# Placement of the expert stage's weight pieces and of its turned activations in SBUF: 32 and 256 bytes past multiples of 512

## The reference, cut to what matters

```python
def swiglu(x, w1, w3, w2):
    return (jax.nn.silu(x @ w1) * (x @ w3)) @ w2

def moe_swiglu(x, router, w1, w3, w2):
    ...
    logits = (xt @ router).astype(F32)
    top_v, top_i = lax.top_k(logits, TOP_K)
    gates = jax.nn.softmax(top_v, axis=-1)
    combine = jnp.sum(jax.nn.one_hot(top_i, N_EXPERTS, dtype=F32) * gates[..., None], axis=1)
    out = jnp.zeros(xt.shape, F32)
    for e in range(N_EXPERTS):
        out = out + combine[:, e:e + 1] * swiglu(xt, w1[e], w3[e], w2[e]).astype(F32)
```

## Time and profile before

| | |
|---|---|
| median of three runs | 1508.27 us |
| profiled execution, its own time | 1508.43 us |
| its span, first to last instruction | 1506.6 us |
| granted TensorE clock, mean over the span | 0.995 |
| PE busy | 1479.1 us (98%) |
| weight loads (PEld) busy | 1297.6 us (86%) |
| DVE busy | 1236.9 us (82%) |
| ACT busy | 962.0 us (64%) |
| read from memory, written | 446.45 MB, 36.87 MB |

### The profile page before, as it was taken

The page is one execution under the profiler, slowest core; times in us unless marked ns, Lnnn a source line. Parts: engine busy times, 40 slices in busy tenths (PEclk is TensorE's granted clock), DMA queues, the critical chain, the costliest instruction groups (busy, mean ns, idle before and its releaser), DMA issues.

```text
span 1506.6 us, 23455 instructions
## 1 busy us (share of the span) xinstructions
PE 1479.1 (98%) x8803; PEld 1297.6 (86%) x8804; DVE 1236.9 (82%) x906; ACT 962.0 (64%) x693; POOL 83.8 (6%) x65
## 2 busy tenths in 40 slices
PE   9998999999999999999999999999999999999997
PEld 8987899999999978888888888888888888888885
DVE  6898866656578779889888888888888888988987
ACT  6644353333353567777777777777777777777774
POOL 1035200000000030000000000000000000000300
PEclk9999999999999999999999999999999999999998
DMA  8745697888654669999999999999999999999990
GB/s 311 225 131 157 221 342 267 305 297 300 228 182 168 228 227 413 403 367 389 376 381 382 373 393 375 377 385 376 382 392 359 387 395 361 388 385 364 407 413 36
DMA packets 212938, 483.97 MB, mean 321 GB/s; under 512 B 8810, under 2 KB 26314, under 8 KB 209820
## 3 DMA queue, kind: packets, MB, share of 16 engines
q1 hardware_dynamic: 209224, 473.67, 85.2%
q10 hardware_dynamic: 2388, 5.32, 1.0%
q0 software_dynamic: 1280, 4.33, 0.7%
HBM read 446.45 MB, written 36.87 MB: 321 GB/s over the span
## 4 chain that ended last, share of the span: by engine, by line
PE 86%; DVE 1%; issue 0%; ACT 0%; DVEq 0%
PE Q L2544 20%; PE Q L2495 14%; PE Q L2497 14%; PE Q L2496 14%; PE Q L2039 7%; PE Q L2040 7%; PE Q L2041 7%; PE Q L2528 2%; DVE wlo L1174 1%; PE Q L2474 0%; PE Q L2505 0%; ACT yrows L1149 0%; PE Q L2400 0%; PE Q L2408 0%; PE Q L2032 0%
## 5 line engine op out<-in xcount | busy, mean ns | idle before, releaser
L1174 DVE TENSOR_TENSOR wlo<-raw,whi 128x2048 fp32r<-128x2048 f32 x413 | 940.3, 2297 | 186.2 <-ACT whi L988 109.3
L988 ACT ACTIVATE whi<-raw 128x2048 fp32r<-128x2048 f32 x336 | 642.2, 1919 | 169.8 <-PE Q L2497 81.1
L2495 PE MATMUL Q<-whi,xgh 128*128 128x512 f32 x896 | 354.2, 395 | 0.0
L2497 PE MATMUL Q<-whi,xgl 128*128 128x512 f32 x896 | 349.6, 390 | 0.0
L2496 PE MATMUL Q<-wlo,xgh 128*128 128x512 f32 x896 | 348.9, 389 | 0.0
L2039 PE MATMUL Q<-xh,whi 128*128 128x264 f32 x1024 | 294.7, 288 | 5.4 <-DVEq L1285 1.8
L2040 PE MATMUL Q<-xl,whi 128*128 128x264 f32 x1024 | 292.0, 285 | 0.0
L2041 PE MATMUL Q<-xh,wlo 128*128 128x264 f32 x1024 | 290.7, 284 | 0.0
L2039 PEld LDWEIGHTS Q<-xh,whi 128*128 128x128 f32 x1024 | 193.8, 189 | 8.1 <-issue 4.1
L2497 PEld LDWEIGHTS Q<-whi,xgl 128*128 128x128 f32 x896 | 168.1, 188 | 35.8
L2496 PEld LDWEIGHTS Q<-wlo,xgh 128*128 128x128 f32 x896 | 168.5, 188 | 33.6
(11 more groups left out here) (286 smaller groups left out, 1138.8 us busy)
## 6 DMA issues: line engine op xcount, KB each, us to landing
raw<-in_moe_w SPq DMA_DIRECT2D x336, 1024.0 KB, 7.1
raw<-in_ffn_w SPq DMA_DIRECT2D x42, 1024.0 KB, 7.3
raw<-in_hgrn_w_in SPq DMA_DIRECT2D x16, 1024.0 KB, 7.3
xg_rows<-zeros SPq DMA_DIRECT2D x6, 2048.0 KB, 10.9
y_rows<-zeros SPq DMA_DIRECT2D x6, 2048.0 KB, 11.7
raw<-in_conv_w_in SPq DMA_DIRECT2D x12, 1024.0 KB, 5.4
raw<-in_hgrn_w_out SPq DMA_DIRECT2D x4, 1024.0 KB, 5.0
raw<-in_conv_w_out SPq DMA_DIRECT2D x4, 1024.0 KB, 5.1
```

The lines of the kernel that those rows point to most:

```text
L988: a.activation(bufs(q)[0], raw[:, n % RAW, PW * (q % 2):PW * (q % 2 + 1)], ACT.Copy).then_inc(hi_done, 1)
L1174: v.tensor_tensor(low, raw[:, slot, PW * half:PW * (half + 1)], high.bitcast(F32), ALU.subtract).then_inc(lo_done, 1)
L2495: t_.matmul(out, xgh[:, kt, :], high[:, w], start=(kt == 0), stop=False)
L2497: mm = t_.matmul(out, xgl[:, kt, :], high[:, w], start=False, stop=(kt == DT - 1))
```

## The change

Two tiles are moved. An unused tile `gap` of 64 floats (256 bytes) goes in ahead of `hth`, so that `hth`, `htl` and the small routing tiles behind them begin 256 bytes later. `hs_at`, from which the places of `hs`, `xg`, `xgh` are counted back, is corrected by the same amount and stays. `W2_AT`, the beginning of `whi2`, is put 32 bytes past the rounded value; the rounding itself gives the same number as before, since another area ends later (`conv_end`). So `whi2` and `wlo2`, and with them all blocks in slots 3 to 5, begin 32 bytes past a multiple of 512, as does `gffn`, which uses part of the same space earlier.

```diff
-        (xs, xgh, xgl, xg, hs, hx, hth, htl), o = region(
+        (xs, xgh, xgl, xg, hs, hx, _, hth, htl), o = region(
             R0, ("xs", [P, TT, D], F32), ("xgh", [P, DT, P], F32R), ("xgl", [P, DT, P], F32R),
-            ("xg", [P, D], F32), ("hs", [P, FW], F32), ("hx", [P, FW], F32),
+            ("xg", [P, D], F32), ("hs", [P, FW], F32), ("hx", [P, FW], F32), ("gap", [P, 64], F32),
             ("hth", [P, 4, P], F32R), ("htl", [P, 4, P], F32R))
-        hs_at = o - 2 * size([P, 4, P], F32R) - 2 * size([P, FW], F32)
+        hs_at = o - 2 * size([P, 4, P], F32R) - 2 * size([P, FW], F32) - size([P, 64], F32)
...
-        W2_AT = (max(o, conv_end) + 511) // 512 * 512
+        W2_AT = (max(o, conv_end) + 511) // 512 * 512 + 32
```

## The result

The median went from 1506.74 us (six runs, 1505.57 to 1510.22) to 1519.69 us (six runs, 1517.25 to 1521.66): a ratio of 1.0086 with a 95% interval from 1.0075 to 1.0097, 13.0 us slower. The forecast was 14.2 us slower. The sign, the place and nearly the size came out as written; the reason given for the price did not, as the experiments show.

A forecast was written before the change was run, and what follows sets the result against it. The prediction took PE's matmul rate in the expert stage to bound the kernel; 1508.43 us plus 14.2 for whi2 and wlo2, all else at nothing, gave 1522.6 us, with an 8-in-10 range of 1507 to 1529.

The forecast's parts named there:

- What bounds the kernel: Expert stage: PE is busy 910.00 of 910.00 us, so a matmul's gain or loss moves the end one for one.
- The price of whi2 and wlo2: Up matmuls in slots 3 to 5: 7.08 ns more on each of 2004, 14.2 us, all on PE.
- The reason: Moving operands come in fixed 64-byte groups, 17 steps each, paid in full; a 32-byte offset touches one more, 7.08 ns.
- G: Moving operands: fixed 64-byte groups, each started one paid in full; 32 bytes off gives 561 steps in place of 544.
- the prediction's own list: Expert matmuls: right if slots 3 to 5 stand at 233 to 236 ns and slot 2 and all of down at 226.7.
- hth and htl: Held operands of 1320 down matmuls, 256 bytes on: costed at 0, bounds 0 to 5.0 ns each (6.6 us).
- The one called faster: Expert matmuls: the offset ends load and stream collisions, 13.4 ns each, 44.5 us less, about 1464 us; chance 0.07.
- The one called slower still: Expert matmuls: load and stream kept from settling, 16.6 us on top of 14.2, about 1539 us; chance 0.08.
- No change: Expert streams: groups counted from the operand's own start, 32 for 512 columns wherever they begin; 1508.4 us, chance 0.30.
- The Trainium skill's rule: SBUF operands: cachelines of 16 bytes with a penalty at each crossing, so the change would cost nothing, 1508.4 us.

The follow-up runs named there:

- everything at 32: whi, wlo, whi2, wlo2, xgh, xgl, hth and htl all 32 bytes past a multiple of 512, against the kernel before: ratio 1.0000 (0.9990 to 1.0009).
- slot 2 with `xgh` at 32: whi2, wlo2, xgh and xgl 32 bytes past a multiple of 512, against the kernel before: ratio 1.0026, slot 2 at 233.3 ns.
- the one kernel with 256 columns: The kernel with whi2, wlo2 at 32 bytes and 8 held columns, up streaming 256 of each 512 columns: slot 2 at 115.8 ns, slot 4 at 112.7.
- the control with 8 held columns: The kernel before, all operands at multiples of 512, with up holding 8 of 128 columns of xgh and xgl: ratio 0.9996 (0.9985 to 1.0006).

## Why the prediction was right in size and wrong in its reason

**What bounds the kernel: right.** PE's distances were the time: of the 12.5 us that the span grew, 11.9 lie between the first up and the last down matmul, and PE has no idle time there (920.00 of 920.00 us from 580 on). DVE and ACT only waited longer (114.3 for 104.9 us, 83.4 for 78.4).

**The price of whi2 and wlo2: near in size.** 7.08 ns were forecast for a matmul; settled runs show 6.0 to 6.9. In a block 36 of them are 255 ns, and 217 were measured. The most of what is missing is in slot 3, the first piece behind the transposes: it was unsettled and dear before the change (231.7 ns), so it lost 33 ns a block where 85 were counted; slots 5 and 4 lost 76 and 80 of 85. The prediction had that row and used it for a bound only. Against it stands a loss that it costed at nothing, the head of down, 27 ns a block, where the offsets change over. It also left out 12 down matmuls of the last expert's last block, whose weights lie in slot 5, which are under 0.1 us.

**The reason: wrong.** The step that failed is the one that reads "512 columns that begin half way into one touch 33 groups, not 32". Streams that begin there cost 226.5 ns if the held operand begins there too (everything at 32: ratio 1.0000), streams that begin at a multiple of 512 cost 233.3 if it doesn't (slot 2 with `xgh` at 32), and at 64 bytes, where G asks nothing, 5.4 us were paid. What the runs show in its place is the difference of the two operands' offsets. A sign of it stood in the result already: by the prediction's own list, down that moves too means load against stream, and the first five matmuls of down moved to 232 ns. That 17 steps for a half-used group fitted both 512 and 264 columns was no proof: I took one rule for both because it gave both numbers, and 121.5 ns was a mean of unequal distances; with `fh` and `fl` at multiples of 512 they come apart into 121.7 and 116.7. The size came out by coincidence.

**hth and htl: right, by the right row.** `yh` against `yl` had the same difference of 256 and no price; 0.9991 and 0.9997 confirm it on either side. That row held only for a settled run, though: the same pairing takes 233 ns at the end of the changed kernel (last section).

**The rivals.** The one called faster had the right variable, the difference of offsets, and the wrong sign: equal offsets were the cheap case already. The one called slower still named the mechanism that the runs support (an offset that keeps load and stream from settling) but put it on top of the groups. "No change" fell with the result. The Trainium skill's rule in "SBUF — State Buffer", section "Specifications (TRN2)", lines of 16 bytes, would have every offset here cost nothing. 233.6 ns at 32 and 229.1 at 64 don't agree with it as the only unit, while everything at 32 does.

**What stays open.** Why the difference matters. It isn't in proportion to what is loaded (231.8 ns with 8 columns), with streams of 256 columns the sign turned, and the same offsets have two prices (233.6 and 229.1 ns by turns with 192; 231.1 ns in a row of 71 and 226.7 afterwards with equal offsets). So the price is that of a state which lasts, and the difference of offsets bears on which state a run falls into. That fits a question of when two reads begin against each other, but no run here shows such a time; this was not settled.

## What to carry to other kernels

Where fp32r matmuls of 512 columns follow one another without idle time, compare the offsets of the held and the streamed operand within 512 bytes: equal ones and those 256 apart were free once a run had settled, others (32, 64, 96, 128, 192) cost 1 to 3.5% of every matmul. Lay both by one rule rather than aligning one of them, and measure again where the streams have another length, since in the one kernel with 256 columns the order was the other way round. And a rule that gives two numbers of a trace isn't yet the cause of them: vary the thing that it says doesn't matter (here, 64 and everything at 32) before using it elsewhere, and look at single distances behind a mean (120.2 ns was two of 121.7 and one of 116.7).

## What the runs showed that was not expected

- The settled price of 512 columns, 226.7 ns or 17 steps of 2.4 GHz for 16 columns, is the same with a load of 128 columns (188 ns) and of 8 (89 ns), so it isn't made by the load.
- A run has to settle: behind the transposes, or where the offsets change over, some five to nine matmuls cost about 232 ns before they reach 226.7. It can fail to settle at all for a long time, as the first up matmuls of the control with 8 held columns show (231.1 ns, 71 in a row).
- At the very end of the changed kernel the twelve matmuls of line 2613, whose own operands did not move, run unsettled behind the last piece in slot 5: 2.10 us for nine of them, 233 ns each, where the earlier trace rows has 226.7.

```profile
1504.56 0.86 PE L2613 MATMUL Q<-yh,pick 128*8 128x512 f32 x3
...
1506.66 0.87 PE L2613 MATMUL Q<-yl,pick 128*8 128x512 f32 x3
```
